# Three chains of three-pass products for the projections of two mixers in a float32 network

## The reference

```python
proj = h @ w_in[layer]
q, k, v, z_attn, xbc, dt_raw, z_ssm = jnp.split(proj, splits, axis=-1)
...
mixed = jnp.concatenate([y_attn, y_ssm], axis=-1) @ w_out[layer]
x = x + gate[:, None, :] * mixed
...
r, k, v = jnp.einsum('nbsd,nde->nbse', xm[:3], w_rkv)
```

## Time and profile before

| | |
|---|---|
| median of 3 runs | 2945.35 us (2941.18 to 2945.79) |
| profiled execution | 2945.46 us, of which the span from first to last instruction is 2943.7 us |
| mean granted PE clock | 0.901 |
| PE busy | 2524.7 us (86%) |
| PE weight load busy | 1888.9 us (64%) |
| DVE busy | 1223.9 us (42%) |
| ACT busy | 736.6 us (25%) |
| transfers | 158.89 MB, mean 54 GB/s |

### The profile page before, as it was taken

The page is one execution under the profiler, slowest core; times in us unless marked ns, Lnnn a source line. Parts: engine busy times, 40 slices in busy tenths (PEclk is TensorE's granted clock), DMA queues, the critical chain, the costliest instruction groups (busy, mean ns, idle before and its releaser), DMA issues. The chain is left out here.

```text
span 2943.7 us, 38477 instructions
## 1 busy us (share of the span) xinstructions
PE 2524.7 (86%) x16824; PEld 1888.9 (64%) x16824; DVE 1223.9 (42%) x1761; ACT 736.6 (25%) x1043; POOL 55.2 (2%) x76
## 2 busy tenths in 40 slices
PE   7899999897899797469987799999862998899997
PEld 7778555376654573169963688878530556688785
DVE  0130332266410432664544466743118333566633
ACT  0231554122300223011011322222210542322222
POOL 0000110000000000012100000000000000000000
PEclk9999999897989898579997799999765999799998
DMA  5222000120112121000001123222030001123220
GB/s 200 83 88 72 0 1 1 57 80 8 51 50 72 57 76 50 0 2 4 4 4 35 46 93 100 94 86 89 9 109 18 0 1 58 50 93 100 85 94 36
DMA packets 45270, 158.89 MB, mean 54 GB/s; under 512 B 5056, under 2 KB 6976, under 8 KB 44720
## 3 DMA queue, kind: packets, MB, share of 16 engines
q1 hardware_dynamic: 43440, 149.71, 15.7%
q10 hardware_dynamic: 1664, 6.73, 0.6%
HBM read 154.28 MB, written 2.14 MB: 53 GB/s over the span
## 5 line engine op out<-in xcount | busy, mean ns | idle before, releaser
L699 PE MATMUL banks<-up_x_high,up_w_high 128*128 128x512 f32 x704 | 275.8, 392 | 20.4 <-DVE up_x_low L712 20.4
L700 PE MATMUL banks<-up_x_low,up_w_high 128*128 128x512 f32 x704 | 275.4, 391 | 0.0
L701 PE MATMUL banks<-up_x_high,up_w_low 128*128 128x512 f32 x704 | 275.3, 391 | 0.0
L269 PE MATMUL banks<-act,weight_ring 128*128 128x512 f32 (+1 forms) x528 | 237.0, 612 | 17.2 <-DVE act L953 12.7
L269 PEld LDWEIGHTS banks<-act,weight_ring 128*128 128x128 f32 (+1 forms) x528 | 102.2, 194 | 155.3 <-issue 152.6
L699 PEld LDWEIGHTS banks<-up_x_high,up_w_high 128*128 128x128 f32 x704 | 133.2, 189 | 51.3 <-issue 23.5
L682 DVE TENSOR_TENSOR up_w_low<-weight_ring,up_w_high 128x1024 fp32r<-128x1024 f32 x88 | 107.7, 1226 | 138.8 <-ACT up_w_high L677 138.8
L720 DVE SCALAR_TENSOR_TENSOR act<-banks,cols,act 128x511 f32<-128x511 f32 (+2 forms) x212 | 158.8, 749 | 7.5
L701 PEld LDWEIGHTS banks<-up_x_high,up_w_low 128*128 128x128 f32 x704 | 133.0, 189 | 27.8
L700 PEld LDWEIGHTS banks<-up_x_low,up_w_high 128*128 128x128 f32 x704 | 133.1, 189 | 27.6
L314 PE MATMUL banks<-down_x_high,down_w_high 128*128 128x512 f32 x352 | 139.4, 396 | 13.1 <-DVE down_x_low L353 13.1
(11 more groups left out here) (373 smaller groups left out, 4672.5 us busy)
## 6 DMA issues: line engine op xcount, KB each, us to landing
weight_ring<-in_up SPq DMA_DIRECT2D x88, 512.0 KB, 3.4
weight_ring<-in_down SPq DMA_DIRECT2D x44, 512.0 KB, 3.4
weight_ring<-in_w_in SPq DMA_DIRECT2D x28, 512.0 KB, 3.4
weight_ring<-in_w_ada SPq DMA_DIRECT2D x24, 512.0 KB, 3.5
weight_ring<-in_w_rkv SPq DMA_DIRECT2D x24, 512.0 KB, 3.4
weight_ring<-in_w_out SPq DMA_DIRECT2D x16, 512.0 KB, 3.4
weight_ring<-in_w_q SPq DMA_DIRECT2D x8, 512.0 KB, 3.4
weight_ring<-in_w_k SPq DMA_DIRECT2D x8, 512.0 KB, 3.4
```

What stands on the lines that cost most here:

```text
L269: mm = nc.tensor.matmul(PS[0:n_cols, n % 4, :], w[:, k % 8 * n_cols:(k % 8 + 1) * n_cols], rhs(k), start=k == 0, stop=k == k_tiles - 1)
L699: nc.tensor.matmul(PS[:, n % 4, :], high, x_high[:, k, :], start=k == 0, stop=False)
L700: nc.tensor.matmul(PS[:, n % 4, :], high, x_low[:, k, :], start=False, stop=False)
L701: mm = nc.tensor.matmul(PS[:, n % 4, :], low, x_high[:, k, :], start=False, stop=k == 7)
```

## The change

A new helper, `split_chain`, takes several products ("jobs") and runs the steps of all of them in one block as one row. The casts of the first step of product g+1 stand ahead of the eight evictions of product g; PE takes up a bank for the new product when `taken` says that the old result has been read. A job can have `tokens=True`: then the tokens are the stationary side and the weights the moving one, so that the result has tokens on the partitions; its eight banks are four blocks of tokens times two halves of the channels.

Three places use it:

- q, k and v of the first block are one chain of 24 steps in one block with the norm ahead of them. v changes from plain float32 to three passes. One block was q with the norm, the next k, a third v.
- the output projection is a chain of one job with 16 steps; it changes from plain float32 to three passes. It stays in one block with the norm ahead of it. DVE takes the eight banks after the last step.
- r, k and v of the time mix are one chain of 24 steps with `prepare`; they were three blocks.

The weights of v and of the output projection come in the other layout (one chunk per contraction step); size and count of the chunks stay. The core of the diff:

```diff
+        def split_chain(name, *jobs):
+            x_high, x_low, w_high, w_low = open_split(name, 7, 2)
...
+            def tensor(pe):
+                for s, (job, k) in enumerate(steps):
+                    g = jobs.index(job)
+                    next_chunk(pe)
+                    pe.wait_ge(wl_made, s + 1)
+                    pe.wait_ge(xl_made, s + 1)
+                    last = k == job["k_tiles"] - 1
+                    for n in range(8):
+                        if k == 0 and g:
+                            pe.wait_ge(taken, 8 * (g - 1) + n + 1)
+                        if job.get("tokens"):
+                            left, right = slice(n // 2 * P, (n // 2 + 1) * P), slice(n % 2 * T, (n % 2 + 1) * T)
+                            nc.tensor.matmul(PS[:, n, :], x_high[:, s % 2, left], w_high[:, s % 2, right], start=k == 0, stop=False)
+                            nc.tensor.matmul(PS[:, n, :], x_high[:, s % 2, left], w_low[:, s % 2, right], start=False, stop=False)
+                            mm = nc.tensor.matmul(PS[:, n, :], x_low[:, s % 2, left], w_high[:, s % 2, right], start=False, stop=last)
...
+            def scalar(act):
+                for s, (job, k) in enumerate(steps):
+                    i = first + s
+                    act.wait_ge(weight_loaded[i % RING], 16 * (i // RING + 1))
+                    if s >= 2:
+                        act.wait_ge(weight_used, i - 1)
+                    nc.scalar.copy(w_high[:, s % 2, :], ring[:, i % RING, :]).then_inc(wh_made, 1)
...
+                    nc.scalar.copy(x_high[:, s % 2, :], job["rhs"](k)).then_inc(xh_made, 1)
+                    for g in range(len(jobs) - 1):
+                        if s == begins[g + 1] and jobs[g]["by"] == "act":
+                            take_all(act, g)
...
+            def vector(dve):
+                def prepare(s):
+                    if s < len(steps) and steps[s][0].get("prepare"):
+                        if s >= 8:
+                            dve.wait_ge(xh_made, s - 7)
+                            dve.wait_ge(xl_made, s - 7)
+                        steps[s][0]["prepare"](steps[s][1]).then_inc(prepared, 1)
...
-        run_stage(norm_in, split_program("q", 8, rows(h), {"act": lambda e, n, b: nc.scalar.mul(q[:, n, :], b, HD ** -0.5)},
-                                         rhs_ready=h_ready))
-        split_gemm("k", 8, rows(h), {"act": copy_act(rows(k_))})
...
-        gemm_tokens("v", 8, lambda k, b: h[:, k, b * P:(b + 1) * P], lambda n: v_tok[:, :, n * P:(n + 1) * P])
+        run_stage(norm_in, split_chain("qkv",
+                  dict(k_tiles=8, rhs=rows(h), ready=h_ready, by="act", take=lambda e, n, b: nc.scalar.mul(q[:, n, :], b, HD ** -0.5)),
+                  dict(k_tiles=8, rhs=rows(h), by="act", take=copy_act(rows(k_))),
+                  dict(k_tiles=8, rhs=rows(h), by="act", tokens=True, take=copy_act(lambda n: v_tok[:, n // 2, n % 2 * T:(n % 2 + 1) * T]))))
...
-        run_stage(norm_ssm, gemm_program("w_out", 8, 16, lambda k: y_attn[:, k, :] if k < 8 else y_ssm[:, k - 8, :],
...
+        run_stage(norm_ssm, split_chain("w_out",
+                  dict(k_tiles=16, rhs=lambda k: y_attn[:, k, :] if k < 8 else y_ssm[:, k - 8, :], by="dve",
...
-            split_gemm(name, 8, rows(xm), {"act": copy_act(rows(dst))}, prepare=mixed(xm, xx, b))
+        run_stage(split_chain("rkv", *(dict(k_tiles=8, rhs=rows(xm), by="act", take=copy_act(rows(dst)), prepare=mixed(xm, xx, b))
+                                       for b, dst in enumerate((r, kx, v)))))
```

More of the change, by code:

```diff
@@ L97, in head_selectors @@
     return one.reshape(KT, P, H).transpose(1, 0, 2).reshape(P, KT * H), one.T
-ORDER = ["xT", "cols", "squares", "late", "bucket1h", "w_ada", "w_q", "w_k", "w_in", "w_z", "w_dt", "w_out", "w_rkv", "w_w1", "w_a1",
+ORDER = ["xT", "cols", "squares", "late", "bucket1h", "w_ada", "w_q", "w_k", "w_v", "w_in", "w_z", "w_dt", "w_out", "w_rkv", "w_w1", "w_a1",
          "w_g1", "w_w2", "w_a2", "w_g2", "w_o", "d_in", "d_uq", "d_widx", "d_uk", "d_uv", "d_qidx", "d_wo", "rel_bias",
@@ L189, in program @@
         planned(A["w_k"], range(8), 8)
-        planned(A["w_in"], range(28), 8)
+        planned(A["w_v"], range(8), 8)
+        planned(A["w_in"], range(20), 8)
         planned(A["w_dt"], range(1), 8, 16)
         planned(A["w_z"], range(8), 8)
-        planned(A["w_out"], range(8), 16)
+        planned(A["w_out"], range(16), 8)
         planned(A["w_rkv"], range(24), 8)
@@ L512, in program @@
         q, k_, v = F[2], F[3], F[4]
-        run_stage(norm_in, split_program("q", 8, rows(h), {"act": lambda e, n, b: nc.scalar.mul(q[:, n, :], b, HD ** -0.5)},
-                                         rhs_ready=h_ready))
-        split_gemm("k", 8, rows(h), {"act": copy_act(rows(k_))})
[L517 to L542, removed]
-        v_tok = v[:, :, :].rearrange("p a b -> p (a b)").rearrange("p (b c) -> p b c", b=NB)
-        gemm_tokens("v", 8, lambda k, b: h[:, k, b * P:(b + 1) * P], lambda n: v_tok[:, :, n * P:(n + 1) * P])
+        v_tok = v[:, :, :].rearrange("p a b -> p (a b)").rearrange("p (b c) -> p b c", b=NB)
+        run_stage(norm_in, split_chain("qkv",
+                  dict(k_tiles=8, rhs=rows(h), ready=h_ready, by="act", take=lambda e, n, b: nc.scalar.mul(q[:, n, :], b, HD ** -0.5)),
+                  dict(k_tiles=8, rhs=rows(h), by="act", take=copy_act(rows(k_))),
+                  dict(k_tiles=8, rhs=rows(h), by="act", tokens=True, take=copy_act(lambda n: v_tok[:, n // 2, n % 2 * T:(n % 2 + 1) * T]))))
+        restore("k")
         checkpoint("v", v[:, :, :])
@@ L927, in program @@
                                              scratch=rows(F[6]))
-        run_stage(norm_ssm, gemm_program("w_out", 8, 16, lambda k: y_attn[:, k, :] if k < 8 else y_ssm[:, k - 8, :],
-             {"dve": lambda e, n, b: nc.vector.scalar_tensor_tensor(out=x[:, n, :], in0=b, scalar=mod[:, 16 + n:17 + n], in1=x[:, n, :],
-                                                                    op0=ALU.mult, op1=ALU.add)},
-             rhs_ready=lambda pe, k: y_ssm_ready(pe, k - 8) if k >= 8 else None))
+        run_stage(norm_ssm, split_chain("w_out",
+                  dict(k_tiles=16, rhs=lambda k: y_attn[:, k, :] if k < 8 else y_ssm[:, k - 8, :], by="dve",
+                       ready=lambda eng, k: y_ssm_ready(eng, k - 8) if k >= 8 else None,
+                       take=lambda e, n, b: nc.vector.scalar_tensor_tensor(out=x[:, n, :], in0=b, scalar=mod[:, 16 + n:17 + n], in1=x[:, n, :],
+                                                                           op0=ALU.mult, op1=ALU.add))))
+        restore("w_out")
         norm("norm_f", rows(x), 8, D, 1e-6, lambda i: col("norm_f_gain", i), rows(x), scratch=rows(F[6]))
@@ L983, in program @@
         differences(xx)
-        for b, (name, dst) in enumerate((("r", r), ("k7", kx), ("v7", v))):
-            split_gemm(name, 8, rows(xm), {"act": copy_act(rows(dst))}, prepare=mixed(xm, xx, b))
+        run_stage(split_chain("rkv", *(dict(k_tiles=8, rhs=rows(xm), by="act", take=copy_act(rows(dst)), prepare=mixed(xm, xx, b))
+                                       for b, dst in enumerate((r, kx, v)))))
+        restore("rkv")
         a_, sig, tmp = F[6:9]
@@ L1755, in lay_out @@
          "w_q": weight_rows(w_in[:, :D]), "w_k": weight_rows(w_in[:, D:2 * D]),
-         "w_in": weight_tiles(w_in[:, 2 * D:at]), "w_z": weight_rows(w_in[:, at + 16:]),
-         "w_dt": weight_tiles(w_in[:, at:at + 16], 16), "w_out": weight_tiles(i["w_out"][0]),
+         "w_v": weight_rows(w_in[:, 2 * D:3 * D]), "w_in": weight_tiles(w_in[:, 3 * D:at]), "w_z": weight_rows(w_in[:, at + 16:]),
+         "w_dt": weight_tiles(w_in[:, at:at + 16], 16), "w_out": weight_rows(i["w_out"][0]),
          "w_rkv": weight_rows(i["rwkv_w_rkv_2"][0]),
```

41 lines of the change are left out of this document (added).

## The result

| | before | after |
|---|---|---|
| median of 4 runs | 2943.39 us (2941.18 to 2945.79) | 2893.39 us (2892.99 to 2893.73) |
| profiled execution | 2945.46 us | 2893.73 us |
| span | 2943.7 us | 2892.0 us |

The ratio of the times is 0.983, with a 95% interval of 0.9813 to 0.9847. The kernel became 50.0 us faster by the medians; the forecast was 50.6 us and 2894.9 us.

The account below looks back on a forecast made before the run. PE, busy 86% of the span, was taken as the bound; gains of 21.9 + 14.5 + 14.2 = 50.6 us off 2945.46 gave 2894.9 us, own range 2890 to 2901, full range 2886 to 2907.

Parts of the forecast that it names:

- q, k, v, 21.9 us: First block's q, k, v as one chain, v in three passes: 21.9 us gained, attention about 0.25 us later behind the last matmul.
- The four terms: In q, k, v: gap q to k 4.35 us, k's slow start 2.88, gap k to v 1.07, v's three passes 13.89.
- Output projection, 14.5 us: Three passes in 16 steps, 87.0 us, after a later, slow start: 14.5 us gained, 14.1 to 15.1 by the slow start.
- The head: Start of the output projection: PE waits for low parts behind DVE's eight normed tiles and starts 7.5 us later.
- the slow start: Output projection: PE, idle beforehand, starts at the lower clock; taken as 2.5 us from 1.95 to 2.93 seen elsewhere.
- r, k, v, 14.2 us: Time mix's r, k, v as one chain: 132.5 us instead of 146.75, 14.2 us gained.
- The seam costs nothing: Between chained products: next product's second step is ready 0.8 us (the cover) before PE wants it, so zero cost.
- Transfers cost nothing: Weight chunks of 512 KB wanted every 5.44 us, 96 GB/s, in v and the output projection: priced at nothing.
- The rivals: Four alternatives: seams not free (0.07), plain products no worse (0.02), slower by the clock (0.02), transfers do the pacing (0.03).
- the clock: Rival 3: PE granted 1.2 GHz for most of the chains; half of their matmuls slow gives 3048.5 us; chance 0.02.
- the fourth rival: Transfers pace v and the output projection, a chunk per 7.15 us, so only seams gain: 2923 us; chance 0.03.
- Stages that the change does not touch: Prediction called itself wrong if the other stages changed by more than 2 us together.

Follow-up runs that it names:

- order: Changed kernel, still three chains, but ACT evicts the old product ahead of the casts for the next product's first step: 2918.5 us.
- v plain: Changed kernel with q and k still chained and v as plain float32 matmuls in a block of its own: 2908.9 us.
- both heads: Kernel with the output projection's first low parts moved ahead of the norm's writes, with the same done to q: 2880.2 us.
- the experiment on the projection's head: Changed kernel, with DVE making the output projection's first-step low parts ahead of the norm's eight writes, PE waiting for these only at bank 5: 2886.0 us.

## Why the prediction was right

It forecast 2894.9 us and 50.6 us gained; 2893.4 and 50.0 were measured. By its steps:

- *q, k, v, 21.9 us*: 22.05 in the trace. The four terms stand by themselves too: without v's three passes +15.5 us (14.7 worked out; 14.8 in the trace), without the seams +12.0 (14.4; 12.5 in the trace, where the slow start of k was 1.54 us and not 2.9).
- *Output projection, 14.5 us*: 14.0 in the trace. The head came out as worked out, 7.5 us, all of it on the path: taking it away gained 7.4. The mis-sized term is the slow start, taken as 2.5 and measured as 3.0; this is just above the highest of before, 2.93. It is no fixed price: at this same place it is 3.0 us in five of the traces in which the stage is unchanged, and 1.4 and 1.5 in the other two (order, v plain), so the stage's bounds of 14.1 to 15.1 were too narrow. That 2.5 was near has some luck in it.
- *r, k, v, 14.2 us*: 14.1 in the trace, 14.0 by undoing it.
- *The seam costs nothing*: right, but the cover was mis-sized. The prediction read 5.36 us for eight evictions as ACT's own pace of 0.67 us and had 0.8 us of cover. That pace was PE's, which finishes a bank every 0.68 us. ACT can do one in 0.48 us, and the cover is 1.86 us.
- *Transfers cost nothing*: right, up to 96 GB/s at clock 1.00 and no wait for a chunk.
- *The rivals*: none came about. For the clock, and with it the rule of the Trainium skill on cycling through the PSUM banks ("TensorE: Matmul & The Clock Gate", the section on psum-queue depth-cycling), the window of 137 to 264 answers: 127 us of banks in turn, with two seams, at 1.00. The rule's brief idle times are not there, and where an experiment made one of 1.54 us at each seam, the clock still held. Two readings in the rivals were off, and nothing hangs on them: a chunk took not 7.15 us in the plain products but 7.18 in v (57.41 / 8) and 6.98 in the projection (111.69 / 16), and the fourth rival's 2923 leaves out that the projection would also have started 7.5 us later.
- *Stages that the change does not touch*: the prediction allowed 2 us together and had no term for them. Aligning the two profiled runs by DVE's instructions, the lead fell from 22.05 us at the start of attention to 20.5 at the norm ahead of the output projection, and rose from 48.6 at the end of the time mix's v to 51.7 at the end. Together that is 1.6 us. The 3.1 gained are all made in the 40 us behind the time mix's v, and half of them in one burst of sixteen records, before and after:

```profile
1154.00 8.49 PE L269 MATMUL banks<-after_conv_act,weight_ring 128*64 128x512 f32 x16 [1.93 <-DVE after_conv_act L953]
```

```profile
1103.74 7.05 PE L270 MATMUL banks<-after_conv_act,weight_ring 128*64 128x512 f32 x16 [1.93 <-DVE after_conv_act L1010]
```

The code and the idle time ahead (1.93 us) are the same; the first 3 us of the burst have clock 0.52 before and 1.00 after. That is 1.4 us; a burst ahead of it has 1.0 (9.87 and 8.91 us, the low level lasts longer before), and an idle time of PE ahead of that one 0.7 (8.35 and 7.69), whose cause is open. Slow starts move in the other runs too: in those with the second or third part undone, q's, untouched, was 1.6 and 1.8 us against 2.5 in the changed kernel. So the time that PE spends at the low level moves from trace to trace where the code is the same; why it moves, no run here shows. Behind these 40 us the lead stays between 50.6 and 53.2 us. The medians, over several runs, show less of it than the pair of profiles: 50.0 against 51.7 us.

## What to carry to other kernels

A seam between two stages costs the length of the pipeline that feeds the bound engine (here two casts and two low parts, 3 us, behind evictions) plus the slow start that its idle time brings; it is removed by putting the next stage's first step ahead of the last stage's evictions in the helpers' queues. Leaving out the barrier alone does little: a seam without it but in the old order cost 6.3 us (25.1 / 4), one with it 7.0 (14.0 / 2). Before a helper's pace is used as its cost, see whether it was waiting for the bound engine between two instructions. And where an engine splits or prepares operands for the bound engine behind other work in its queue, look for the first step's operands that don't depend on that work.

## What was not expected of the hardware

In the products of this study, idle times of PE of 0.92 us (k to v before; 1.07 from the end of the last matmul's slot), 1.33 and 1.54 us were followed by matmuls at the full clock level, those of 3.58 us (both heads), 3.68 and more by matmuls at the low one. In between, the length of the idle time alone does not tell: 1.93 us were followed by the low level in the trace of before and by the full one in that of the changed kernel, ahead of the same matmuls (the rows of 1154.00 and 1103.74 above). Nor is the fall always there at once: behind an idle time of 3.87 us in the changed kernel (a burst at 1469.90, behind the time mix) the first 1.1 us had clock 0.96 and the next 3 us 0.50. And a product can begin at the low level with no idle time just ahead, when PE had done little before (810.43 in the experiment on the projection's head). ACT read a PSUM bank of 128x512 every 0.48 us when nothing made it wait.
